# One core of Trainium2, a two-layer diffusion step with expert retrieval: GpSimd issues the last stage's rows without waiting for earlier ones to land, from places that open earlier

## The chip, the cores and the metric

The kernel runs on one core of a Trainium2 chip. The metric is the device time of one execution in microseconds. The engines are named as the profile names them: PE (TensorE), DVE (VectorE), ACT (ScalarE), POOL (GpSimd) and SP (SyncE, which here only starts transfers).

## What is computed

The reference is one inference step of a backbone with two layers. Each layer runs over a context of 128 tokens and over 256 latent tokens, width 1024, in f32. A layer mixes tokens (pooling windows, a scan, attention) and then retrieves experts:

```python
def peer_ffn(h, lp):
    ...
    q = (xt @ lp["peer_wq"]).reshape(n_tok, PEER_HEADS, 2, PEER_HALF)
    s = jnp.einsum("thmd,mhnd->thmn", q, lp["peer_keys"]).astype(jnp.float32)
    v1, i1 = lax.top_k(s[:, :, 0], PEER_TOPK)
    v2, i2 = lax.top_k(s[:, :, 1], PEER_TOPK)
    ...
    top_s, pos = lax.top_k(cand_s, PEER_TOPK)
    idx = jnp.take_along_axis(cand_i, pos, axis=-1)
    ...
        act = jnp.einsum("td,thkd->thk", xb, u_tab[ib])
        return jnp.einsum("thk,thkd->td", jax.nn.gelu(act) * gb, v_tab[ib])
```

Every token picks 128 of 16384 experts (8 heads, 16 each). For each pick it needs a row u of 1024 numbers (a dot product with the token, then gelu and gate) and a row v of 1024 numbers (added up with that weight). The pooling mixer subtracts each token from its mean over windows of 2, 4, 8 and 16 tokens. The outputs are the normed tokens and the new keys, values and scan states.

## The kernel before, in words

**Steps.** The program is four steps k = 0 to 3: context and latent of layer 0, context and latent of layer 1. A tile is 128 tokens, one per partition; a latent step has two tiles. A step has a dense part (projections, mixers, scores, the choice of experts) and a gather part. The gather part of a step lies partly beside the dense part of the next: `gather_plans` writes, for each named pause of the dense part, which gather events each engine does there, and `run_beside` carries that out on PE, ACT and DVE alike. `BESIDE_LATENT` is such a table: "s6" at the pause ("choose", 1, 0) means that share 6 of the weights is made there, "v24" that PE adds up four rows there.

**Rows and places.** POOL issues one indirect transfer per pick: it brings for each of the 128 tokens one row of the expert table (L825). For context steps these are single rows ("u" and "v", 128x1024); for latent steps they are double rows ("f", 128x2048), u and v side by side, about 1 MB a transfer. The last step has 256 of them, f0 to f255. A row lands in a place: a piece of `ring` (five double places), or memory that a stage doesn't need and lends with `spare_line` between two positions of the stream: pieces of `work`, `lent_line`, `wring[1]`. In the last step the order of places is worked out once, when the program is built; a row takes the free place that was used longest ago.

**What POOL waits for.** Before a row it waits (a) until the row that held the place before has been used: `u_used` counts dot products on DVE, `v_used` sums on PE; (b) for what the first use of a lent place names; (c) for a bound on rows under way, `UNDER_WAY = 8` in single rows: with a double row, the row five before it must have landed (`landed_first`, semaphores `row_landed...`). In the last step f0 to f4 go to the ring. The three double places in `work` open at `after_step[3]`, that is with row 11 of the step, and wait for `cleaned`: ACT multiplies the old contents by zero (`L.worn`, L1622) after the second tile's experts are chosen (`picked`), since the last step leaves out some rows. `lent_line` opens at row 8, two double places in `wring[1]` at row 52, two more at row 174.

**Last step.** Its first 24 x 128 experts are not gathered; they are computed densely: PE jobs "ua" (L1243, weights `peer_us`), a selection (L1257, L2243 and L2245 with the small table `count`), and sums "n" (L1271, weights `peer_vs`, 12 loads of 1 MB into two halves of `wring[0]`). For the picks that fall there the indirect transfer has an index out of bounds and moves nothing.

**A row's way.** DVE takes the dot product (L2229), ACT the gelu of two of them (L1630), DVE makes the weights of the two rows (L2185, L2193: `cond<-const,wv`), PE adds both up (L1287, `acc<-...,cond`), which frees the places. The engines run the events in the order of the plan; `events_two` writes it.

**SP.** At the end it loads `final_norm_w` for the context tile into hn[2], and later once more for the latent tiles into mod_a, then `count`, then `peer_vs`. Earlier it loads the band matrices of the pooling mixer, 128x2048 in a latent step, which PE multiplies at L1030 (one 256-column product for each of four windows and two tiles).

## Time and profile before

| | us |
|---|---|
| median of 3 runs | 2503.35 (2500.39 to 2504.37) |
| time of the profiled execution | 2499.15 |
| its span | 2497.0 |
| busy PE, DVE, POOL, ACT in the span | 1817.0, 1628.9, 999.7, 358.8 |

```profile
DMA  9989999979889999999999999987997999999997
GB/s 382 406 349 357 385 397 328 351 307 368 299 355 422 423 415 421 421 416 422 422 390 421 383 403 374 352 333 283 351 345 285 383 377 396 374 365 376 391 395 281
...
q0 software_dynamic: 147456, 740.81, 75.5%
q1 hardware_dynamic: 19490, 187.93, 18.4%
```

The span is cut into 40 slices of 62.4 us; a digit of DMA is the busy share of the 16 DMA engines in tenths. The lower two lines are queues: packets, MB and share; q0 carries POOL's rows, q1 what SP starts. The last step's rows are added up from about 1892 us to 2485 us, slices 31 to 40.

### The profile page before, as it was taken

Reading aid. Unit: us, or ns where it says so; the run is one execution under the profiler, and the core shown is the slowest. Engines: PE = TensorE matmul, PEld = TensorE weight load, DVE = VectorE, ACT = ScalarE, POOL = GpSimd, SP = SyncE. Lnnn points to the kernel's source line nnn. Section 1 sums busy time; section 2 is a strip of 40 time slices with the busy share of each in tenths; the row PEclk is TensorE's granted clock in tenths of the full one; section 3 lists DMA queues with packets and bytes.
Section 4 is the critical chain, followed back from the end, with each engine's and each line's share of the span. In section 5 each row is a group of like instructions: output and inputs, shape, how many; then the busy total and the mean of one; then the engine's idle time right before and its main releaser. Section 6 shows DMA issues by size and latency. Waiting matters only on the chain.

```text
span 2497.0 us, 24844 instructions
## 1 busy us (share of the span) xinstructions
PE 1817.0 (73%) x7834; PEld 840.7 (34%) x7834; DVE 1628.9 (65%) x4613; ACT 358.8 (14%) x1003; POOL 999.7 (40%) x1028
## 2 busy tenths in 40 slices
PE   6899656778447576676646796677985978778995
PEld 2455432354112221123311264235641533333221
DVE  0348984574785456564588689456666669887557
ACT  1321132101010122210001113211111000000000
POOL 0004536544533233333333555644453445444343
PEclk9899788978678787888977898787997989989998
DMA  9989999979889999999999999987997999999997
GB/s 382 406 349 357 385 397 328 351 307 368 299 355 422 423 415 421 421 416 422 422 390 421 383 403 374 352 333 283 351 345 285 383 377 396 374 365 376 391 395 281
DMA packets 167076, 930.31 MB, mean 373 GB/s; under 512 B 26311, under 2 KB 28871, under 8 KB 97007
## 3 DMA queue, kind: packets, MB, share of 16 engines
q0 software_dynamic: 147456, 740.81, 75.5%
q1 hardware_dynamic: 19490, 187.93, 18.4%
q8 instruction: 62, 1.02, 0.2%
q14 instruction: 68, 0.56, 0.1%
HBM read 990.08 MB, written 3.15 MB: 398 GB/s over the span
## 4 chain that ended last, share of the span: by engine, by line
DMA 31%; PE 29%; DVE 18%; issue 14%; another core or an unknown queue 4%; ACT 3%; POOL 1%; SPq 0%; POOLq 0%; DVEq 0%; ACTq 0%
DMA ring<-peer_uv_in,vidx 14%; DMA work<-peer_uv_in,vidx 11%; PE psum L1193 7%; PE acc L1287 5%; PE acc L1309 3%; PE psum L917 3%; DMA wring<-peer_uv_in,vidx 2%; DVE work L2229 2%; DVE ring L2281 2%; DVE work L1733 1%; PE psum L944 1%; PE psum L1243 1%; DVE work L1728 1%; PE acc L843 1%
## 5 line engine op out<-in xcount | busy, mean ns | idle before, releaser
L825 POOL DMA_INDIRECT ring<-peer_uv_in,vidx x428 | 419.2, 979 | 598.8 <-PE acc L1287 194.8
L1287 PE MATMUL acc<-ring,cond 128*32 128x512 f32 x984 | 294.0, 709 | 225.0 <-DVE cond L2193 222.7
L825 POOL DMA_INDIRECT ring<-peer_uv_in,idx x193 | 182.8, 947 | 379.5 <-DVE idx L1865 201.9
L825 POOL DMA_INDIRECT work<-peer_uv_in,vidx x207 | 205.4, 992 | 285.2 <-PE acc L1287 99.2
L2229 DVE CUSTOM_DVE_ANT_0 work<-work,h_kept 128x1024 f32<-128x1024 f32 (+1 forms) x183 | 221.2, 1218 | 98.3 <-DMA work<-peer_uv_in,vidx 92.3
L1287 PE MATMUL acc<-work,cond 128*32 128x512 f32 x732 | 213.3, 695 | 67.3 <-DVE cond L2193 66.3
L2281 DVE CUSTOM_DVE_ANT_0 ring<-ring,h_kept 128x1024 f32<-128x1024 f32 x193 | 224.1, 1216 | 8.5 <-DMA ring<-peer_uv_in,idx 4.1
L2229 DVE CUSTOM_DVE_ANT_0 ring<-ring,h_kept 128x1024 f32<-128x1024 f32 x128 | 153.9, 1218 | 75.5 <-DMA ring<-peer_uv_in,vidx 59.2
L1193 PE MATMUL psum<-work,wring 128*128 128x256 f32 (+1 forms) x896 | 172.8, 353 | 29.2 <-issue 26.2
L1287 PEld LDWEIGHTS acc<-ring,cond 128*32 128x32 f32 x984 | 53.0, 122 | 414.2 <-DVE cond L2193 262.6
L1630 ACT ACTIVATE dots<-dots 128x2 f32<-128x2 f32 x256 | 51.9, 203 | 917.4 <-DVE dots L2229 911.6
L2229 DVE CUSTOM_DVE_ANT_0 work<-ring,h_kept 128x1024 bf16<-128x1024 f32 x118 | 142.5, 1217 | 54.0 <-DMA ring<-peer_uv_in,vidx 39.0
L1309 PE MATMUL acc<-ring,lent_line 128*32 128x512 f32 x728 | 126.3, 700 | 66.5 <-DVE lent_line L2176 34.7
L1193 PEld LDWEIGHTS psum<-work,wring 128*128 128x128 f32 x896 | 148.7, 201 | 58.2 <-issue 39.0
L1351 ACT ACTIVATE work<-psum 128x512 f32<-128x512 f32 (+3 forms) x226 | 94.5, 429 | 509.8 <-PE psum L1193 150.6
L917 PE MATMUL psum<-wring,work 128*128 128x512 f32 (+1 forms) x400 | 153.6, 540 | 10.1 <-ACT work L1382 5.7
L1287 PEld LDWEIGHTS acc<-work,cond 128*32 128x32 f32 x732 | 41.7, 122 | 211.5 <-issue 106.2
L1728 DVE MAX8 work<-work 128x8 f32<-128x128 f32 (+1 forms) x288 | 52.5, 253 | 83.5 <-ACT work L1351 67.4
L917 PEld LDWEIGHTS psum<-wring,work 128*128 128x128 f32 x400 | 72.2, 198 | 92.3 <-issue 84.9
L825 POOL DMA_INDIRECT lent_line<-peer_uv_in,vidx x57 | 56.3, 987 | 92.9 <-PE acc L1287 46.7
L1271 PE MATMUL psum<-wring,work 128*128 128x512 f32 x192 | 92.9, 620 | 0.0
L1243 PE MATMUL psum<-work,wring 128*128 128x256 f32 x384 | 88.8, 385 | 0.3 <-issue 0.3
(280 smaller groups left out, 2674.5 us busy)
## 6 DMA issues: line engine op xcount, KB each, us to landing
wring<-w_in_in SPq DMA_DIRECT2D x17, 2048.0 KB
wring<-peer_wq_in SPq DMA_DIRECT2D x14, 2048.0 KB
wring<-mod_w_in SPq DMA_DIRECT2D x10, 2048.0 KB
ring<-mod_w_in SPq DMA_DIRECT2D x9, 2048.0 KB, 11.8
wring<-w_out_in SPq DMA_DIRECT2D x8, 2048.0 KB
wring<-peer_us_in SPq DMA_DIRECT2D x6, 2048.0 KB
wring<-peer_vs_in SPq DMA_DIRECT2D x12, 1024.0 KB, 9.3
work<-mod_w_in SPq DMA_DIRECT2D x5, 2048.0 KB, 14.1
```

Source lines behind the costliest of these rows:

```text
L825: nc.gpsimd.indirect_dma_start(row(kind, k, t, r)[0], None, io["peer_both" if kind == "f" else "peer_one"], bass.IndirectOffsetOnAxis(ap=a ...
L917: ins = mm(p[:, 0:n], st.L.hT[0][:, b, t * P:(t + 1) * P], w[:, b, slot:slot + n], start=(b == 0), stop=(b == DB - 1))
L1193: ins = mm(p[:, 0:N], chunk("wq", k, b // 4)[:, kb, (b % 4) * P:(b % 4 + 1) * P], st.L.hT[1][:, kb, 0:N], start=(kb == 0), stop=(kb == DB ...
L1243: ins = mm(p[:, 0:st.N], w[:, b, i % PER_CHUNK * P:(i % PER_CHUNK + 1) * P], st.L.hT[1][:, b, 0:st.N], start=(b == 0), stop=(b == DB - 1))
L1271: ins = mm(bank("vd", k, 2 * t + half)[:, :], steps[k].L.expert_acts[:, i, t * P:(t + 1) * P], shared_v(part)[:, at:at + CHUNK], start=(i ...
L1287: ins = mm(acc[half][lane:lane + QUAD, :], vw_duo(k, t, i)[:, j * QUAD:(j + 1) * QUAD], held[:, D + half * CHUNK:D + (half + 1) * CHUNK], ...
L1309: ins = mm(acc[half][lane:lane + QUAD, :], w[:, at:at + QUAD], two[j - pair][0][:, half * CHUNK:(half + 1) * CHUNK], start=(r == 0), stop= ...
L1351: A(dst, src, ACT.Copy, scale=scale).then_inc(*take(*key))
L1630: A(dots[:, at:at + DUO], dots[:, at:at + DUO], ACT.Gelu_apprx_tanh).then_inc(*mark("gelu", k, t, i))
L1728: d(V.max(top[:, b * TOPK + 8 * r:b * TOPK + 8 * r + 8], values[:, b * width:(b + 1) * width]))
L2229: V.tensor_tensor_reduce(st.L.products[i % 2] if st.dense else held[:, 0:D], held[:, 0:D], h_kept[:, :], 1.0, 0.0, ALU.mult, ALU.add, dots ...
L2281: V.tensor_tensor_reduce(held, held, h_kept[:, :], 1.0, 0.0, ALU.mult, ALU.add, dots[:, dots_at(k, t) + r:dots_at(k, t) + r + 1]).then_inc ...
```

## The change

It has seven parts.

1. In the last step POOL does not wait for an earlier row to have landed: `if n in landed_first and not steps[k].dense`. In the other steps it still does.
2. Places of the last step: the three double places in `work` and `lent_line` open at row 5 or 8 (`INDEXED_ROW`, `CLEANED_ROW`) in place of 11 and 8. Two of them (10D to 14D) wait for `both_indexed` of the second tile and for the first `cleaned`; the third (8D to 10D) for `picked` of the second tile and the second `cleaned`. The places behind, and how many there are, stay as they were.
3. ACT's cleaning is cut in two events "c": the first, 128x1512, at the pause ("choose", 1, 0), the second, 128x2048, at ("exp", 1). Before, two of 128x2048 came with the event "S".
4. Shares 6 and 7 of the context step's weights are made earlier, at ("choose", 0, 7) and ("choose", 1, 0) in place of ("choose", 1, 0) and ("choose", 1, 2).
5. On DVE and POOL's list, row f2's dot product comes behind the weights of rows 0 and 1.
6. The bands of a latent step shrink from 2048 to 1088 columns (`REACH` = 136): only the part of each window matrix that is not zero is loaded and multiplied. PE does 12 products (136, 16 and 120 columns) where it did 8 of 256.
7. SP: the final norm's weights are loaded once, into hn[2], and used for all three tiles. In step 0 the first chunk of `peer_wq` is loaded behind the states' output and the keys, not ahead of them.

```diff
+REACH = 128 + max(POOL_WINDOWS) // 2
...
+INDEXED_ROW, CLEANED_ROW = 5, 8
...
-            L.band = region(10776, 2048)
+            L.band = region(10776, 8 * REACH)
...
-                L.worn = [region(8 * D, 2 * D), region(12 * D, 2 * D)]
+                L.worn = [region(12824, 14 * D - 12824), region(8 * D, 2 * D)]
...
-        spare_line(region(10 * D, 2 * D), 2, after_step[STEPS - 1], len(stream))
-        for worn in steps[STEPS - 1].L.worn:
-            spare_line(worn, 2, after_step[STEPS - 1], len(stream))
+        indexed_used, cleaned_used = row_no["f", STEPS - 1, 0, INDEXED_ROW], row_no["f", STEPS - 1, 0, CLEANED_ROW]
+        spare_line(region(10 * D, 4 * D), 4, indexed_used, len(stream))
+        spare_line(region(8 * D, 2 * D), 2, cleaned_used, len(stream))
...
-        line_from = {k: row_no["f", k, 0, LENT_ROW] for k in (1, 3)}
+        line_from = {1: row_no["f", 1, 0, LENT_ROW], 3: row_no["f", 3, 0, INDEXED_ROW]}
...
-                    load_chunk("wq", k, 0)
...
                 for cc in range(4):
-                    if k or cc:
-                        load_chunk("wq", k, cc)
+                    load_chunk("wq", k, cc)
...
-                if st.lat:
-                    sp.wait_ge(*after("h2", st.k, st.T - 1))
-                else:
+                if not st.lat:
...
-                if n == after_step[STEPS - 1]:
-                    pool.wait_ge(*after("cleaned"))
+                if n == indexed_used:
+                    pool.wait_ge(*after("both_indexed", STEPS - 1, 1))
+                    pool.wait_ge(*after("cleaned", 0))
+                if n == cleaned_used:
+                    pool.wait_ge(*after("picked", STEPS - 1, 1))
+                    pool.wait_ge(*after("cleaned", 1))
...
-                if n in landed_first:
+                if n in landed_first and not steps[k].dense:
                     pool.wait_ge(*row(*stream[landed_first[n]])[1:])
...
+                        near, far = (st.L.band[:, (g * T + ti) * REACH:(g * T + ti + 1) * REACH] for ti in range(T))
+                        both = 2 * REACH - N
+                        mm(to[:, 0:REACH], held[0], near, start=True, stop=False)
+                        mm(to[:, N - REACH:REACH], held[1], far[:, 0:both], start=False, stop=True)
+                        ins = mm(to[:, REACH:N], held[1], far[:, both:], start=True, stop=True)
...
+                if kind == "c":
+
+                    act.wait_ge(*after("picked", k, i))
+                    worn = steps[k].L.worn[i]
+                    A(worn, worn, ACT.Copy, scale=0.0).then_inc(*mark("cleaned", i))
...
+BESIDE_DENSE = {("choose", 0, 7): "v23 s6", ("choose", 1, 0): "v24 v25 s7", ("choose", 1, 2): "v28 v29"}
...
+            if steps[k].dense:
+                plan["choose", 1, 0] = plan["choose", 1, 0] + [("c", k, 0, 0)]
+                plan["exp", 1] = plan["exp", 1] + [("c", k, 1, 1)]
+                third = left.pop(left.index(("f", k, 0, 2)))
+                left.insert(left.index(("p", k, 0, 0)) + 1, third)
```

**POOL at the start of the last step's rows**, in the kernel before. A row is an instruction: line, kind, place and table, shape, and the semaphores it waits for; `row_landed` with a number is the landing of an earlier row, `v_used` the sums on PE. The first row is f0:

```order
L825 DMA ring<-peer_uv_in,vidx 128x2048 [waits v_used,row_landed45,both_indexed]
L825 DMA ring<-peer_uv_in,vidx 128x2048 [waits row_landed2,v_used]
...
L825 DMA ring<-peer_uv_in,vidx 128x2048 [waits row_landed4,v_used]
L825 DMA lent_line<-peer_uv_in,vidx 128x2048 [waits v_used,row_landed6,mod_whole]
...
L825 DMA work<-peer_uv_in,vidx 128x2048 [waits row_landed2,cleaned,picked]
```

And in the changed kernel, from f0:

```order
L829 DMA ring<-peer_uv_in,vidx 128x2048 [waits v_used,both_indexed]
L829 DMA ring<-peer_uv_in,vidx 128x2048 [waits v_used] x4
L829 DMA work<-peer_uv_in,vidx 128x2048 [waits v_used,mod_whole,cleaned,both_indexed]
L829 DMA work<-peer_uv_in,vidx 128x2048
L829 DMA lent_line<-peer_uv_in,vidx 128x2048 [waits v_used]
L829 DMA work<-peer_uv_in,vidx 128x2048 [waits cleaned,picked]
L829 DMA ring<-peer_uv_in,vidx 128x2048 [waits v_used] x2
```

Rows f5 to f8 have moved from ring and `lent_line` places, which wait for sums of this step's own rows, to `work` and `lent_line`, which wait for none of them; the waits for landings are gone from every row of the step.

**DVE while the last step's experts are chosen**, before (L1871 is the end of the first tile's choice, L1886 waits for ACT's exp, L2176 makes a share of weights):

```order
L1871 COPY vidx<-idx 32x32 x15
L1880 COPY small<-work 128x8
L1882 TENSOR_TENSOR work<-work,small 128x128 [waits v_step]
L1886 TENSOR_REDUCE small<-work 128x8 [waits topk_exp]
...
L1740 MATCH_REPLACE work<-work 128x128 x15
L2176 TENSOR_TENSOR lent_line<-const,wv 128x512 [waits v_used,v_step]
```

and in the changed kernel:

```order
L1882 COPY vidx<-idx 32x32 x15
L1891 COPY small<-work 128x8
L1893 TENSOR_TENSOR work<-work,small 128x128 [waits v_step]
L2187 TENSOR_TENSOR lent_line<-const,wv 128x512 [waits v_used]
L1897 TENSOR_REDUCE small<-work 128x8 [waits topk_exp]
...
L1751 MATCH_REPLACE work<-work 128x128 x15
L2187 TENSOR_TENSOR lent_line<-const,wv 128x512 [waits v_used,v_step]
```

Share 6 now stands ahead of the wait for `topk_exp`, and share 7 where share 6 was.

**DVE at the last step's first rows**, before (L2309 ends the context tile's sum, the ISA rows are dot products, L2185 and L2193 make the weights of rows 0 and 1):

```order
L2309 TENSOR_TENSOR x2<-x2,acc1 64x512 x2
L2229 ISA work,dots<-ring,h_kept 128x1024 [waits x_new,v_step,u_used,row_landed4]
L2229 ISA dots 128x1
L2185 TENSOR_TENSOR wv<-dots,idx 128x2 [waits gelu]
L2193 TENSOR_TENSOR cond<-const,wv 128x64 [waits v_used,v_step]
```

and in the changed kernel:

```order
L2320 TENSOR_TENSOR x2<-x2,acc1 64x512 x2
L2196 TENSOR_TENSOR wv<-dots,idx 128x2 [waits x_new,v_step,gelu]
L2204 TENSOR_TENSOR cond<-const,wv 128x64 [waits v_used,v_step]
L2240 ISA work,dots<-ring,h_kept 128x1024 [waits u_used,row_landed4]
L2240 ISA dots 128x1
```

The dot product of f2 has moved behind the weights that PE waits for.

## Rows read from the trace of the kernel before

**Rows 1.** Windows: length, busy PE, PEld, DVE, ACT, POOL; clock, DMA share, GB/s.
```profile
1905.00:1950.00 45.00, 34.43 (x146) 18.31 (x147) 24.58 (x53) 3.56 (x15) 20.53 (x21) 0.92 0.96 367
1950.00:2200.00 250.00, 200.17 (x943) 94.21 (x941) 195.52 (x444) 14.89 (x65) 117.65 (x113) 0.91 0.98 383
2100.00:2200.00 100.00, 80.30 (x404) 37.04 (x404) 85.75 (x189) 5.67 (x24) 50.64 (x48) 0.92 0.97 380
2200.00:2300.00 100.00, 81.78 (x383) 33.24 (x384) 87.45 (x195) 5.29 (x26) 48.15 (x46) 0.92 0.95 363
2300.00:2480.00 180.00, 158.24 (x480) 46.62 (x476) 111.22 (x248) 7.52 (x37) 71.28 (x71) 0.96 0.98 390
```

**Rows 2.** The chain that ended last: the first of nine row transfers, 2092 to 2188 us.
```profile
2092.09 8.71 DMA ring<-peer_uv_in,vidx
```

**Rows 3.** POOL's line, 2090 to 2190 us: whom it waited for, us, times.
```profile
  PE acc L1287: 17.2, 15
  DMA ring<-peer_uv_in,vidx: 13.7, 10
  DMA work<-peer_uv_in,vidx: 8.4, 7
```

**Rows 4.** Windows in which the DMA engines had little to do.
```profile
1840.00:1850.00 10.00, 6.20 (x32) 1.35 (x32) 9.93 (x64) 0.00 (x0) 3.06 (x4) 0.51 0.49 179
1890.00:1905.00 15.00, 4.35 (x11) 1.14 (x11) 11.62 (x30) 4.04 (x4) 1.25 (x2) 0.52 0.26 88
```

**Rows 5.** Timeline of POOL: a slow issue, f4 and f5; start, duration, [idle before].
```profile
1873.41 2.88 POOL L825 DMA_INDIRECT ring<-peer_uv_in,vidx  x1 [0.30 <-issue]
...
1887.01 0.99 POOL L825 DMA_INDIRECT ring<-peer_uv_in,vidx  x1 [0.30 <-issue]
1903.03 0.99 POOL L825 DMA_INDIRECT ring<-peer_uv_in,vidx  x1 [15.03 <-PE acc L1287]
```

**Rows 6.** Timeline of DVE and ACT: both_indexed, picked, f2's dot product, the cleaning.
```profile
1883.34 0.29 DVE L1865 SCALAR_TENSOR_TENSOR idx<-work 128x128 uint32<-128x128 f32 x1
...
1888.90 0.29 DVE L1897 SCALAR_TENSOR_TENSOR cond<-work 128x128 f32<-128x128 f32 x1
...
1898.61 1.22 DVE L2229 CUSTOM_DVE_ANT_0 work<-ring,h_kept 128x1024 bf16<-128x1024 f32 x1 [0.28 <-DVE x L2309]
...
1895.11 3.69 ACT L1622 ACTIVATE work<-work 128x2048 f32<-128x2048 f32 x2
```

**Rows 7.** Timeline of PE: wait for share 6, the last context rows, the first sums.
```profile
1843.80 1.06 PE L1309 MATMUL acc<-ring,lent_line 128*32 128x512 f32 x1 [6.90 <-DVE lent_line L2176]
...
1882.94 1.94 PE L1309 MATMUL acc<-ring,lent_line 128*32 128x512 f32 x8 [2.60 <-DMA ring<-peer_uv_in,vidx]
...
1900.32 3.63 PE L1287 MATMUL acc<-ring,cond 128*32 128x512 f32 x8 [11.74 <-DVE cond L2193]
```

**Rows 8.** SP's transfers at 2005 to 2030 us: count, KB each, us from issue to landing.
```profile
y_prompt_out<-x SPq DMA_DIRECT2D x1, 512.0 KB, 4.5
mod_a<-final_norm_w_in SPq DMA_DIRECT2D x1, 512.0 KB, 9.5
...
work<-count_in SPq DMA_DIRECT2D x1, 64.0 KB, 11.4
```

**Rows 9.** Waits of 2000 to 2300 us: who, for whom, us, times, longest.
```profile
DVE work L2243 <- DMA work<-count_in: 9.6, 1, 9.6
```

**Rows 10.** SP's transfers at 2290 to 2430 us, and the first and last issue among them.
```profile
wring<-peer_vs_in SPq DMA_DIRECT2D x10, 1024.0 KB, 9.2
...
2297.12 11.27 SPq L641 DMA_DIRECT2D wring<-peer_vs_in  x2
...
2421.27 0.33 SPq L641 DMA_DIRECT2D wring<-peer_vs_in  x1
```

**Rows 11.** The band products of step 3, in the chain that ended last.
```profile
1511.25 3.71 PE psum L1030 x16
```

**Rows 12.** Step 0: issue of the first chunk of peer_wq, and PE's use of it.
```profile
148.68 0.33 SPq L657 DMA_DIRECT2D wring<-peer_wq_in  x1
...
164.34 10.98 PE L1193 MATMUL psum<-work,wring 128*128 128x128 f32 x96 [0.80 <-ACT work L1351]
```

More of the change, by code:

```diff
@@ L168, in shape_constants @@
             bands.append(b.reshape(length // P, P, length).transpose(1, 0, 2).reshape(P, -1))
-    lat = np.concatenate(bands[:4], 1).astype(np.float32)
+    lat = np.concatenate([band[:, ti * 2 * P:(ti + 1) * 2 * P][:, ti * (2 * P - REACH):][:, :REACH]
+                          for band in bands[:4] for ti in range(2)], 1).astype(np.float32)
     ctx = np.concatenate(bands[4:], 1).astype(np.float32)
@@ L1028, in dense @@
                         g = 2 * pair + r
[L1029 to L1031 removed]
+                        to = p[64 * r:64 * r + 64, :]
+                        held = [st.L.pz[ti][:, g * 64:(g + 1) * 64] for ti in range(T)]
+                        if T == 1:
+                            ins = mm(to[:, 0:N], held[0], st.L.band[:, g * N:(g + 1) * N], start=True, stop=True)
+                            continue
+                        near, far = (st.L.band[:, (g * T + ti) * REACH:(g * T + ti + 1) * REACH] for ti in range(T))
[3 more added lines that the diff above has]
+                        ins = mm(to[:, REACH:N], held[1], far[:, both:], start=True, stop=True)
                     ins.then_inc(*made("pl", k, pair))
@@ L1618, in gather @@
                 if kind == "S":
-                    if t == 0:
-                        act.wait_ge(*after("picked", k, 1))
-                        for j, worn in enumerate(steps[k].L.worn):
-                            ins = A(worn, worn, ACT.Copy, scale=0.0)
-                        ins.then_inc(*mark("cleaned"))
                     act.wait_ge(*after("picked", k, 1))
```

13 lines of the change are left out of this document (5 added, 8 removed).

## The prediction

> **What bounds the kernel now.** I read the slices first: in the last quarter of the span no compute engine is full and the DMA engines are at nine tenths almost throughout. Then the windows of the last stage [rows 1]: the DMA share is 0.96 to 0.98 from 1905 to 2200 us and again from 2300 to 2480 us, PE stands at 77 to 88% and DVE at 55 to 87%. Then the chain that ended last [rows 2]: from 2092 to 2188 us it is nine row transfers of about 9 us, one issued when the one five before it has landed, so about 2 us a row. That looks like a limit on rows under way, and POOL's waits name it too [rows 3]: 22 us in 100 for landings in the two rows shown, against 17.2 us for places. But with the DMA engines 97% busy at that time, a landing comes late because the engines are full, not because too little is asked of them. What an unbounded queue can win there is the missing 3%. From 2200 to 2300 us the share is 0.95 and the chain goes through DVE (dot product, selection, dot product): DVE sets the pace there, all places are full, and no queue helps.
>
> The last view is the windows with a low share [rows 4]: from 1890 to 1905 us the engines are 26% busy, 11.1 us of nothing; from 1840 to 1850 us 49% busy, 5.1 us. The cause of the first is in POOL's timeline [rows 5]: f0 to f4 fill the five ring places by 1888 us, and f5 is issued at 1903.03 after an idle 15.03 us, released by PE's first sum, which starts at 1900.32 [rows 7].
>
> So I keep the account in DMA time. The last stage must move a fixed number of bytes; it ends earlier by what the engines are spared or are kept busy more, as long as PE and DVE can follow.
>
> **The change part by part.**
>
> *Four rows earlier (parts 2 and 3).* f5, f6 and f7 need both_indexed, which DVE marks at 1883.6 us [rows 6], the end of the context rows' sums, 1884.9 us [rows 7], and the first cleaning, done long before; f8 needs the end of the choice, 1889.2 us, and the second cleaning, half of 3.69 us [rows 6], so about 1891. POOL needs 1.3 us an issue [rows 5], so all four are issued by 1893 us, when the kernel before stood idle until 1903. f9 then waits for ring place 0, as f5 did. Nine rows are there or under way at 1903 us where five were. A row costs the DMA engines 100 us x 0.97 / 48 = 2.02 us [rows 1], so four rows are **8.1 us**. Bounds: 0, if the stage were not bound by DMA; 11.1 us, the whole idle time of that window. I take 8.1, since the share right behind it is 0.96. Can PE and DVE follow? From 1905 to 1950 us PE is 77% busy and DVE 55% [rows 1], waiting for rows; with four rows more in hand these waits close. The cleaning moves on ACT and is smaller (1512 and 2048 columns for twice 2048); ACT is idle there: 0.
>
> *Shares 6 and 7 earlier (part 4).* PE waits 6.90 us for share 6 [rows 7], which starves POOL of places and makes the half-idle 1840 to 1850 us [rows 4]. Its removal brings the last context rows and f0 to f4 some 5 us forward. DVE's choice, on which the next step hangs, doesn't wait for them, and only nine places exist: I give it **0** beyond what it does for the four rows, namely that the queue is empty when f5 comes. If it counts in full it is 5.1 us, below nothing only by the 0.7 us that a share takes on DVE.
>
> *f2 behind the weights (part 5).* PE's first sum waits for DVE, and one dot product of 1.22 us [rows 6] leaves its front: ring place 0 comes free 1.2 us earlier while the DMA engines have nothing: **1.2 us**, bounds 0 and 1.2.
>
> *No bound on rows under way (part 1).* Nothing is added; a wait goes. What is late next is the place (PE's sum). The idle shares outside DVE's stretch are 0.04 x 45 + 0.02 x 250 + 0.02 x 180 = 10.4 us [rows 1]. The bound asks for a row to be whole, that is for the slowest of 16 engines, and the indices out of bounds spread the load unevenly from row to row; with up to nine or eleven rows queued in place of five a fast engine runs dry less often. But some of the idle time is places. Ends: 0 and 10.4; I take half, **5.2 us**.
> The Trainium skill (DMA: Bandwidth & Descriptors, Latency and other measured facts) says that two of the sixteen engines are usually slower than the rest. By that rule the slow ones would set the pace whatever the depth, this term would be 0 and the sum 12.1 us; no row here tells engines apart, and it is the second case below.
>
> *The second load of the norm's weights (part 7)* is 0.5 MB of 390 GB/s: **1.3 us** of DMA time. Also `count` stands behind it in SP's queue: they land 9.5 and 11.4 us after their issue [rows 8], and DVE waits 9.6 us for `count` [rows 9]. It will be about 5 us sooner (4.5 us for the output ahead of it, then 1.9, the difference of the two). DVE gains 4.9 us, but rows go on landing meanwhile and the DMA share is 0.98: **0**, at most 4.9.
>
> *The bands (part 6).* In step 3 the products stand in the chain, 3.71 us [rows 11]. Columns go from 2048 to 1088, to 0.53, instructions from 8 to 12: about 2.0 us, so up to 1.7 us; the loads shrink by 0.5 MB twice, 1.3 us each. Both lie before other waits. Bounds 0 and 3.0, I take **1.5**.
>
> *peer_wq in step 0.* It is issued at 148.68 us and used at 164.34 [rows 12]. Now it goes out about 1.7 us later and behind 1 MB of keys, 2.6 us. A 1 MB load lands in 9.2 us under full load [rows 10]; 2 MB add 2.6 us: 150.4 + 11.8 = 162.2. Covered by 2 us, so **0**; if the cover were short, 2 to 3 us lost.
>
> **Sum:** 8.1 + 1.2 + 5.2 + 1.3 + 1.5 = 17.3 us. The profiled execution took 2499.15 us (span 2497.0), so the same one would take 2481.9. The median of the runs is 4.2 us above the profiled one; from it: 2503.35 - 17.3 = **2486.0 us**.
>
> One thing could spoil the first term. One of POOL's issues takes 2.88 us in place of 0.99 while DVE works on 2048 columns [rows 5]. The new issues fall into DVE's copies of the indices; there f4's took 0.99. Should all four take 2.88, the last would be out at about 1897 us and landed before f9's place is free, a loss of 1 to 3 us.
> The Trainium skill (SBUF — State Buffer, two separate sides) has this as a rule: DVE's f32 copies lock GpSimd out of a shared port, and its transfers starve. By it the slow case holds, and the sum is 15 us.
>
> **The rivals.**
>
> *Depth is worth nothing, part of the rest is absorbed.* The idle 2 to 4% is unevenness that no depth cures, and the four rows bring only what PE's clock and ACT let through. For it: the share is near full. Gain 8 to 12 us, 2493 us.
>
> *All is recovered.* DVE's stretches start earlier by the count's 4.9 us as well and the share goes to 1.00: 17.3 + 5.2 + 4.9 = 27 us, 2476 us. Against it: both can't be had in full, since DMA and DVE take turns.
>
> *The lead is lost.* The four rows only fill places sooner, and DVE's stretch from 2200 us, 87% busy with its waits on ACT and PE between, or PE's from 1930 to 2000, sets the end. Gain under 5 us, 2501 us. Against: DVE's stretch starts only when a DMA-bound one ends [rows 2].
>
> *SP's loads stand behind the deep queue* (slower). If a load had to wait for all rows queued ahead of it, its landing would grow with the depth. peer_vs has two halves, and loads follow each other every (2421.27 - 2297.12) / 9 = 13.8 us [rows 10]; it lands in 9.2 us. From a landing above 13.8 us PE stops at each of ten loads. With nine rows at 2 us ahead, 18 us: 10 x 4.2 = 42 us lost, 2528 us with the gains taken off. Against it: with five rows, 10 us of work, under way, the 0.5 MB output landed in 4.5 us [rows 8], so the two queues take turns.
> The Trainium skill (DMA: Bandwidth & Descriptors, Queues, rings and completion order) says so too: each DMA engine goes round its queues packet by packet. The row agrees, and by the rule this case is excluded.
>
> *The change doesn't do what it says.* POOL may be held by the places at once, so that no more than five are ever under way. Then term 5.2 is 0, which is the first rival.
>
> **How the numbers follow.** A measurement of this kernel can tell about 0.2%, 5 us, from no change. Chances: forecast (2480 to 2490) 0.57; first rival 0.20; all recovered 0.10; lead lost 0.09; slower 0.04. Faster by over 0.2% is 0.87, within 0.2% 0.09, slower 0.04. The range leaves out the slower case and the edge of the others: from 2475 (all recovered) to 2500 (nearly all of the lead lost).
>
> **What would show it.** In the profile after: f5 to f8 issued between 1884 and 1893 us, POOL's wait ahead of f9 down to some 8 us, the share from 1890 to 1905 us near 0.7; no wait of 6.9 us for share 6; no landings among POOL's releasers in the last step, places in their stead; DMA share 0.98 to 0.99 where it was 0.96 to 0.98; DVE's wait for count near 5 us; vs loads landing in 9 to 10 us. I am wrong if the shares stay and the end moves by less than 8 us, if POOL's issues grow long (its descriptors find no room), or if PE waits for peer_vs.

## The result, and the profile after it

The changed kernel takes 2490.66 us (median of 20 runs, 2479.32 to 2509.22), the kernel before, run beside it, 2508.96 us (median of 20, 2498.27 to 2521.19). The measured ratio is 0.9935, with a 95% interval of [0.9917, 0.9953]: 16.3 us faster, 12 to 21 (the two medians alone are 18.3 us apart). The forecast was 17.3 us faster, and 2486.0 us as a time. The time came out 4.7 us above that, inside the stated range of 2475 to 2500 but just outside its likeliest part, 2480 to 2490, because the forecast started from a median of three runs, 2503.35 us, that lies 5.6 us below the median of 20.

Single executions of one kernel lie up to 19 us from their median, so two profiled ones can't be subtracted: the one of the changed kernel took 2494.02 us (span 2492.1) and was already 12.2 us behind at the last step's first peer_us load (1768.72 us, 1756.53 in the kernel before), although the code up to there differs in little. I therefore measure from two marks that every profile has: **approach**, from that load's issue to PE's first sum of the last stage, and **stage**, from that sum to the end of the span. Before: 143.8 and 596.7 us. After: 139.7 and 583.7 us.

Windows of the kernel after, for [rows 1, 4]; the columns are as there.

```profile
1852.20:1862.20 10.00, 5.74 (x32) 3.22 (x32) 8.58 (x54) 0.00 (x0) 6.49 (x7) 0.98 1.01 405
1898.11:1913.11 15.00, 4.46 (x11) 1.14 (x11) 12.72 (x34) 2.93 (x6) 4.25 (x5) 0.51 0.68 245
...
1840.00:1850.00 10.00, 10.00 (x64) 6.80 (x60) 8.12 (x50) 4.69 (x7) 3.96 (x6) 1.00 1.04 416
1890.00:1905.00 15.00, 1.56 (x2) 0.00 (x0) 13.21 (x49) 4.25 (x6) 6.00 (x7) 0.50 0.93 330
...
2100.00:2200.00 100.00, 83.90 (x372) 37.64 (x372) 78.74 (x171) 5.15 (x22) 46.52 (x43) 0.83 0.94 369
2200.00:2300.00 100.00, 83.99 (x385) 34.08 (x386) 88.88 (x198) 5.28 (x26) 52.86 (x50) 0.92 0.93 361
2300.00:2400.00 100.00, 95.84 (x284) 29.45 (x283) 53.14 (x116) 4.07 (x20) 41.29 (x43) 0.98 1.01 413
2400.00:2480.00 80.00, 66.37 (x207) 18.23 (x207) 58.27 (x132) 3.66 (x18) 25.78 (x26) 0.91 0.86 345
```

The same times on the clock don't hold the same work here: the changed kernel is 12.2 us late at the load and 8.1 us late at the first sum, so its rows for 1840 and 1890 us show work that the kernel before did 8 to 12 us earlier. The first two rows are the matching stretches, shifted by 12.2 us for the first hole and laid from 10.3 us ahead of the first sum to 4.7 us behind it for the second. The first hole is closed, 1.01 for 0.49. The second is narrowed: 0.68 for 0.26, near the 0.7 that was foretold, so 4.8 us of idle time are left of 11.1; the 0.93 of the unshifted row is no measure of it. From 2300 to 2400 us the engines move 413 GB/s; the same window of the kernel before reads

```profile
2300.00:2400.00 100.00, 92.93 (x275) 28.71 (x272) 53.82 (x119) 3.86 (x19) 38.61 (x39) 0.98 0.98 391
```

From 2200 to 2300 us, DVE's stretch, nothing is gained, as the prediction had it. The last row of the first fence is new: 0.86 near the end, where the kernel before has 0.97 from 2400 to 2480 us, because the last rows have landed by about 2470 us and the rest of that window has nothing to move.

The bytes show the four rows too. From the load to the first sum the engines of the kernel before move 324 GB/s over 143.8 us, 46.6 MB, and those of the kernel after 356 GB/s over 139.7 us, 49.7 MB; from the first sum to the end it is 368 GB/s and 219.6 MB before, 370 GB/s and 216.0 MB after. Three to four megabytes have moved ahead of the first sum.

POOL's timeline of the kernel after, for [rows 5]: f3 to f9.

```profile
1890.36 0.99 POOL L829 DMA_INDIRECT ring<-peer_uv_in,vidx  x1 [0.30 <-issue]
1891.65 0.99 POOL L829 DMA_INDIRECT ring<-peer_uv_in,vidx  x1 [0.30 <-issue]
1896.85 0.99 POOL L829 DMA_INDIRECT work<-peer_uv_in,vidx  x1 [4.21 <-DVE vidx L1882]
1898.15 0.99 POOL L829 DMA_INDIRECT work<-peer_uv_in,vidx  x1 [0.30 <-issue]
1899.44 0.99 POOL L829 DMA_INDIRECT lent_line<-peer_uv_in,vidx  x1 [0.30 <-issue]
1901.55 1.00 POOL L829 DMA_INDIRECT work<-peer_uv_in,vidx  x1 [1.12 <-ACT work L1630]
1911.12 0.99 POOL L829 DMA_INDIRECT ring<-peer_uv_in,vidx  x1 [8.57 <-PE acc L1299]
```

f5 to f8 go out at 1896.85 to 1901.55 us (12.2 us less for the late start: 1884.7 to 1889.4), one wait each for the index copies (DVE, L1882, which mark both_indexed) and for the second cleaning, and 8.57 us ahead of f9 in place of 15.03 ahead of f5. PE's wait for share 6 is gone: from 1820 to 1880 us none of its waits in the kernel after names DVE. PE's first sum:

```profile
1908.41 3.63 PE L1299 MATMUL acc<-ring,cond 128*32 128x512 f32 x8 [16.84 <-DVE cond L2204]
```

Waits of POOL in the kernel after, 1950 to 2400 us (us, times, longest): no landing among the long ones, places throughout.

```profile
POOL ring L829 <- PE acc L1299: 88.8, 40, 5.1
POOL work L829 <- PE acc L1299: 60.4, 23, 7.7
POOL ring L829 <- issue: 17.8, 50, 0.7
POOL lent_line L829 <- PE acc L1299: 16.0, 8, 6.4
POOL wring L829 <- PE acc L1299: 14.7, 12, 2.2
```

What an unbounded queue does to one row, in the chain that ended last of the kernel after: its three transfers from 2300 to 2400 us. In the kernel before there are six in that stretch, of 9.1 to 15.9 us (the nine of about 9 us that the prediction went by stood from 2092 to 2188 us).

```profile
2304.64 25.63 DMA ring<-peer_uv_in,vidx
...
2348.16 24.04 DMA ring<-peer_uv_in,vidx
...
2386.52 22.56 DMA work<-peer_uv_in,vidx
```

A row takes 23 to 26 us from issue to landing, and the kernel is faster. DVE waits 1.8 us for count, 9.6 before [rows 9]:

```profile
DVE work L2254 <- DMA work<-count_in: 1.8, 1, 1.8
```

### The profile page after: what moved, and what is told of

The parts are those of the page before. It is cut to its first block, busy times and chain, and to the rows that moved or that the text cites. A ratio compares the mean times of both kernels' runs of the same rounds, so it can differ in the third digit from the quotient of the medians.

```text
span 2492.1 us, 24631 instructions
## 1 busy us (share of the span) xinstructions
PE 1832.2 (74%) x7850; PEld 845.1 (34%) x7850; DVE 1629.4 (65%) x4613; ACT 358.0 (14%) x1003; POOL 1004.0 (40%) x1028
## 3 DMA queue, kind: packets, MB, share of 16 engines
q1 hardware_dynamic: 19346, 186.42, 18.3%
## 4 chain that ended last, share of the span: by engine, by line
PE 29%; DMA 27%; DVE 22%; issue 12%; another core or an unknown queue 5%; ACT 3%; POOL 1%; SPq 0%; DVEq 0%; POOLq 0%; ACTq 0%
DMA ring<-peer_uv_in,vidx 14%; DMA work<-peer_uv_in,vidx 9%; PE acc L1299 7%; PE psum L1205 6%; PE psum L921 3%; DVE ring L2292 2%; DVE work L1744 2%; DVE work L2240 2%; PE psum L948 2%; DVE work L1739 2%; PE acc L1321 1%; PE psum L1255 1%; DMA wring<-peer_uv_in,vidx 1%; DVE work L1751 1%
## 5 line engine op out<-in xcount | busy, mean ns | idle before, releaser
L1299 PE MATMUL acc<-work,cond 128*32 128x512 f32 x740 | 219.5, 701 | 65.9 <-DVE cond L2204 64.2
L1321 PE MATMUL acc<-ring,lent_line 128*32 128x512 f32 x728 | 121.0, 689 | 52.5 <-DVE lent_line L2187 27.3
L2196 DVE TENSOR_TENSOR wv<-dots,idx 128x2 f32<-128x2 f32 x256 | 40.0, 156 | 83.3 <-ACT dots L1641 81.5
```

What stands on the lines that cost most here:

```text
L1299: ins = mm(acc[half][lane:lane + QUAD, :], vw_duo(k, t, i)[:, j * QUAD:(j + 1) * QUAD], held[:, D + half * CHUNK:D + (half + 1) * CHUNK], ...
L1321: ins = mm(acc[half][lane:lane + QUAD, :], w[:, at:at + QUAD], two[j - pair][0][:, half * CHUNK:(half + 1) * CHUNK], start=(r == 0), stop= ...
```

## The experiments

All of them were timed in five rounds; a1 to a4 share their runs of the kernel before, as do the repeated kernel and b1 to b3, and d1 to d3 and c1, which ran on another chip. Their intervals are 0.2 to 0.35% wide to each side, 5 to 9 us, so each verdict takes the stage and the approach of the profile with it. All in one table:

| kernel | ratio to before [95%] | approach | stage |
|---|---|---|---|
| before | 1 | 143.8 | 596.7 |
| changed | 0.9935 [0.9917, 0.9953] | 139.7 | 583.7 |
| changed, again | 0.9926 [0.9899, 0.9953] | 139.3 | 576.5 |
| a1: bound back | 0.9937 [0.9903, 0.9971] | 139.3 | 590.7 |
| a2: before + bound off | 1.0007 [0.9977, 1.0036] | 142.5 | 591.4 |
| a3: places late | 0.9958 [0.9927, 0.9988] | 144.1 | 591.4 |
| a4: shares late | 0.9928 [0.9900, 0.9956] | 143.9 | 583.3 |
| b1: second norm load | 0.9943 [0.9922, 0.9964] | 139.0 | 586.5 |
| b2: whole bands | 0.9908 [0.9882, 0.9934] | 139.8 | 583.5 |
| b3: bound of 3 rows | 1.0403 [1.0380, 1.0426] | 139.7 | 696.3 |
| d1: bound back, places late | 0.9960 [0.9936, 0.9985] | 138.5 | 599.2 |
| d2: bound off and places alone | 0.9945 [0.9915, 0.9974] | 143.0 | 580.9 |
| d3: bound of 4 rows | 1.0017 [0.9992, 1.0043] | 140.3 | 607.3 |
| c1: no bound anywhere | 0.9938 [0.9907, 0.9969] | 140.3 | 578.5 |

**How far one profile carries.** The changed kernel, unedited.

> The changed kernel once more, unedited, to see how far one profile's stages can be trusted. 'Stage' here is the time from the issue of the first peer_us load of the last step to the end of the span: 740.5 us in the kernel before, 723.4 in the changed one, 730.0 with the bound back, 733.9 with the bound off alone, 735.5 with the places late, 727.2 with the shares late. If the stage repeats to 2 us (727 or less, 721 or more), the differences of 4 to 12 us between these profiles are effects of the edits; if it comes out at 728 or more, single profiles can't carry them. Ratio to the kernel before 0.9935 again, within 0.003.

It came out at 715.8 us (139.3 + 576.5), 7.6 less than its first profile: below the limit of 721 that I had set. The approach repeats to 0.4 us, the stage does not. With the kernels that have both the absent bound and the places (changed twice, a4, b1, b2, d2, c1) the stage reads 576.5 to 586.5 us, mean 581.8: a single one is good to some 5 us.

**Bound back (part 1 undone).**

```diff
-                if n in landed_first and not steps[k].dense:
+                if n in landed_first:
```

> The changed kernel with the bound of five rows under way put back in the last stage (part 1 undone), all else as changed. The changed kernel is 16 us faster than the one before (ratio 0.9935). Prediction's theory (depth is worth half of the idle shares, 5 us): 11 us faster than the kernel before, ratio 0.9955, and in the stretch from 2300 to 2400 us the DMA engines move about 391 GB/s again as in the kernel before, where the changed kernel moved 413; POOL's releasers are landings again. Rival 'depth is worth nothing' (the rate would follow the rows that the stage happens to ask for): ratio stays at 0.9935, and the rate there stays above 405. Rival 'depth is nearly the whole gain' (the rate rose by 5%, so 5% of some 280 us of full DMA engines, 14 us): ratio 0.998 to 1.000. If the loads of peer_vs stood behind the deep queue, PE's waits on them would shrink here; none is seen in the changed kernel, so no change is expected.

Windows of this kernel, in the same columns:

```profile
1890.00:1905.00 15.00, 7.78 (x26) 2.85 (x27) 11.66 (x23) 0.79 (x3) 3.16 (x5) 0.64 0.67 244
...
2300.00:2400.00 100.00, 95.00 (x282) 29.12 (x281) 54.90 (x121) 4.07 (x20) 39.54 (x40) 0.98 0.98 394
```

The rate is back at 394 GB/s, so it follows the depth and not the rows asked for, and landings are POOL's releasers again:

```profile
POOL ring L829 <- DMA work<-peer_uv_in,vidx: 28.7, 16, 3.2
```

The stage is 8.9 us over the mean of the seven kernels with both parts. But the runs show a ratio of 0.9937, no loss against 0.9935 and 0.9926; 0.9955 lies inside the interval too. This profile started its peer_us load within 0.2 us of the kernel before, and shows the share of 0.67 that was foretold for 1890 to 1905 us (near 0.7), without any shift.

**Bound off alone.** The same line, changed in the kernel before.

> The kernel before with nothing changed but that POOL keeps no bound on rows under way in the last stage (part 1 alone). Prediction's theory: 5 us faster, ratio 0.998; f5 still goes out at about 1903 us (places alone hold it), and the rows after 1910 us are issued as places come free. Rival 'depth is worth nothing': within 1 us, ratio 1.000, DMA rate from 2300 to 2400 us at 391 GB/s. Rival 'depth is nearly the whole gain': 12 to 15 us faster, ratio 0.9945, the rate at 413 GB/s. Rival 'places limit it anyway' (change does not do what it says): single rows would take no longer than the 9 us of the kernel before from issue to landing, where the changed kernel shows 15 to 25 us.

```profile
2300.00:2400.00 100.00, 95.58 (x284) 29.00 (x284) 53.85 (x118) 3.86 (x19) 41.53 (x42) 0.98 1.01 413
```

The rate is 413 GB/s without any other part, and the stage 5.3 us shorter than before. The runs show 1.0007: the expected 0.998 is just inside, 12 to 15 us are out.

**Places late (part 2 undone).**

```diff
-INDEXED_ROW, CLEANED_ROW = 5, 8
+INDEXED_ROW, CLEANED_ROW = 11, 11
...
-        line_from = {1: row_no["f", 1, 0, LENT_ROW], 3: row_no["f", 3, 0, INDEXED_ROW]}
+        line_from = {1: row_no["f", 1, 0, LENT_ROW], 3: row_no["f", 3, 0, LENT_ROW]}
```

> The changed kernel with rows f5 to f8 given no places of their own before f11 (part 2 undone: the double places of indexed_used, cleaned_used and the lent line are used from row 11 on), all else as changed. Prediction's theory (four rows are 8.1 us of DMA time): 8 us slower than the changed kernel, that is 8 us faster than the kernel before, ratio 0.9967; the stretch from 1890 to 1905 us shows a DMA share near 0.3 again. Rival 'the lead is lost' (rows earlier only fill places sooner, DVE or PE sets the end): ratio 0.9935 as the changed kernel, though the hole at 1890 to 1905 us is back. Rival 'the hole counts in full and the first sums are delayed too' (11 us and more): ratio 0.998 or above.

The hole is back, here as POOL's wait ahead of f5, and as the stretch that matches 1890 to 1905 us of the kernel before:

```profile
1903.33:1918.33 15.00, 4.46 (x11) 1.16 (x11) 12.69 (x35) 3.29 (x6) 1.27 (x2) 0.50 0.06 8
...
1916.35 0.99 POOL L829 DMA_INDIRECT ring<-peer_uv_in,vidx  x1 [23.72 <-PE acc L1299]
```

It is deeper than before, a share of 0.06 where near 0.3 was expected. A likely reason is that with the shares made early (part 4) the rows ahead of it have landed sooner, which leaves 3 us more of idle time for the four rows to fill. The stage is 9.6 us over the mean of the seven, the ratio 0.9958. Both stand nearer to 8 us of loss than to none; the lost-lead rival falls by the stage, the runs alone would leave it open. Its approach of 144.1 us is the one outlier of that column, and I have no cause for it.

**Shares late (part 4 undone).**

```diff
-    texts = BESIDE_LATENT | BESIDE_EARLY if early else BESIDE_LATENT | BESIDE_OPENING | {"dt": "u11"} | BESIDE_DENSE
+    texts = BESIDE_LATENT | BESIDE_EARLY if early else BESIDE_LATENT | BESIDE_OPENING | {"dt": "u11"}
```

> The changed kernel with the shares 6 and 7 of the gated and summed rows beside the choice left where they were before (part 4 undone). Prediction's theory (worth 0): ratio 0.9935 as the changed kernel, though PE waits some 7 us for share 6 again and the DMA share from 1840 to 1850 us is near 0.5. Rival 'counts in full': the time from the issue of the first peer_us load to PE's first sum of the last stage is 4 us longer (143.8 us before, 139.7 after), and the ratio is 0.995.

PE's longest wait from 1820 to 1880 us of this kernel, as in [rows 7]:

```profile
PE acc L1321 <- DVE lent_line L2187: 6.9, 1, 6.9
```

The wait is back as expected. The share came out at 0.66, not near 0.5, in the stretch that matches 1840 to 1850 us (1847.80 to 1857.80 us here). The approach is 143.9 us. It is 142.5 to 143.9 in all four kernels with the late shares (before, a2, a4, d2) and 138.5 to 140.3 in nine of ten with the early ones: the rival was right, the part brings the first sum forward by 4 us. Whether the end follows can't be read: the ratio says no, and 4 us are inside its interval. The kernel also settles the rival on SP's queue. Its transfers, with no bound on rows:

```profile
wring<-peer_vs_in SPq DMA_DIRECT2D x12, 1024.0 KB, 9.1
```

The kernel before has 9.3 us in that row of its page. A load doesn't stand behind 25 us of rows.

**Second norm load.** 0.5 MB ahead of count, unused.

```diff
+                    sp.wait_ge(*after("h2", st.k, st.T - 1))
+                    load(mod_a[:, :], final_w, "fw_in", "again")
                     sp.wait_ge(*after("picked", st.k, st.T - 1))
                     load(st.L.count, io["count"], "count_in")
```

> The changed kernel with the last step's second load of the norm's weights (0.5 MB) put back ahead of count, into a tile that nobody reads afterwards. Prediction's theory: 1.3 us of DMA time and DVE's wait for count longer by some 5 us (1.8 us in the changed kernel, 7 to 8 here), worth 0 to 4.9 us, so the stage (first peer_us load to the end) is 1 to 3 us longer than 723.4 and the ratio 0.994. Rival 'the wait for count counts in full': the choice after it and the rows behind are late by the whole 5 us, stage 729 to 730, ratio 0.996.

```profile
DVE work L2256 <- DMA work<-count_in: 10.1, 1, 10.1
```

The wait is 10.1 us, longer than expected; the ratio 0.9943 and stage 586.5 (4.7 over the mean) fit 1 to 3 us and don't exclude 5. Over all profiles the wait for count is 7.8 to 11.1 us with the load (before, a2, b1, d2) and 1.8 to 7.3 us, mean 5.1, without it (ten): "near 5" holds only as a mean.

**Whole bands (part 6 undone).** The matrices of 256 columns a block are loaded and multiplied again, in two matmuls in place of three.

```diff
-            L.band = region(10776, 8 * REACH)
+            L.band = region(10776, 2048)
...
-                        mm(to[:, 0:REACH], held[0], near, start=True, stop=False)
-                        mm(to[:, N - REACH:REACH], held[1], far[:, 0:both], start=False, stop=True)
-                        ins = mm(to[:, REACH:N], held[1], far[:, both:], start=True, stop=True)
```

> The changed kernel with the whole bands of the pooling windows loaded and multiplied (part 6 undone: 2048 columns for 1088, 0.5 MB more in each latent step). Prediction's theory: 1.5 us, ratio 0.994; nothing changes behind the first peer_us load of the last step, so the stage is 723 to 725 us as in the changed kernel. Rival (all 3 us of it count, and more where the loads stand before the first dense work): ratio 0.9955; the stage still the same.

0.9908, the lowest ratio of all, though more work is done. Its interval overlaps that of the changed kernel, so I don't call it faster; but 3 us of loss are excluded and 1.5 lies at the edge: the term is about 0.

**Bound of three double rows.** The last stage's limit at half its value.

```diff
-            while behind and under_way + size[stream[behind - 1][0]] <= UNDER_WAY:
+            most = 4 if stream[n][1] == SHARED_STEP else UNDER_WAY
+            while behind and under_way + size[stream[behind - 1][0]] <= most:
...
-                if n in landed_first and not steps[k].dense:
+                if n in landed_first:
```

> The changed kernel with a bound in the last stage of three double rows under way, where the kernel before has five and the changed one none. Theory 'depth fills the DMA engines': the rate in the stretch from 2300 to 2400 us went from 391 GB/s (bound of five) to 413 (none); with three it falls to 350 or less, and the stage is 745 us or more (11% fewer bytes a second over the 280 us in which the engines are full is 30 us, part of it hidden), ratio 1.003 to 1.01. Rival 'the end hangs on PE and DVE, depth only moves the same bytes forward': the rate falls but the stage grows by no more than the 7 us that the bound of five costs it, ratio below 0.998.

```profile
2300.00:2400.00 100.00, 82.07 (x263) 27.10 (x264) 54.73 (x119) 3.67 (x18) 37.05 (x38) 0.90 0.92 327
```

The rival falls. 327 GB/s, a stage of 696.3 us and 4.0% more than the kernel before: far above what I expected of the first theory, whose direction is right. Depth is worth much here as long as it is scarce. In its chain (22 transfers from 2100 to 2400 us) a row lands in 5.2 to 10.0 us.

**Both large parts undone, and both alone.** d1 joins the edits of a1 and a3; d2 joins those of a4, b1 and b2, puts f2 back before the weights and the first chunk of peer_wq of step 0 back ahead of the keys.

```diff
-                third = left.pop(left.index(("f", k, 0, 2)))
-                left.insert(left.index(("p", k, 0, 0)) + 1, third)
...
                     modulation(MOD_AT["mid"])
+                    load_chunk("wq", k, 0)
```

> The changed kernel with both large terms undone together: the bound of five rows is back and rows f5 to f8 have no places before f11; the small parts 4 to 7 stay as changed. Prediction's sum (5.2 + 8.1 = 13.3 us of 17.3 gone): 4 us faster than the kernel before, ratio 0.9984. Rival 'the two terms overlap' (each undone alone showed 0 to 8 us over the changed kernel in whole runs, but they serve the same rows): with both gone the loss is larger than the sum of the two, ratio 1.000. Rival 'the small parts carry most of it' (shares and f2 earlier, count sooner; a loss of only some 5 us here): ratio 0.995.

> The complement: the changed kernel with parts 4 to 7 undone (shares 6 and 7 and f2 where they were, whole bands, the second load of the norm's weights ahead of count, peer_wq's first chunk of step 0 early), so that of the change only the absent bound and the four places are left. Prediction's sum: 13.3 us faster than the kernel before, ratio 0.9947, and the first peer_us load to first sum takes 143 to 144 us as before. Rival 'the small parts carry most of it': ratio 0.998. Rival 'the small parts are worth nothing together': ratio 0.993 as the changed kernel.

d1's windows show the hole (0.07 of share; its first sum is 1.9 us behind that of the kernel before) and the old rate:

```profile
1890.00:1905.00 15.00, 2.81 (x8) 0.64 (x8) 13.58 (x40) 4.25 (x6) 0.10 (x1) 0.50 0.07 28
...
2300.00:2400.00 100.00, 95.41 (x283) 29.22 (x282) 54.49 (x117) 4.07 (x20) 38.79 (x40) 0.98 0.98 391
```

d2 is where the sum put it, 0.9945 for 0.9947. d1 is at 0.9960 for 0.9984: by it the parts 4 to 7 carry 10 us of 16 rather than 4, though 0.9984 is still inside the interval. d2, which leaves them out, is only 2 to 5 us slower than the changed kernel. The stage of d1, 599.2 us, is near that of the kernel before (596.7), as it should be with both parts gone; the parts 4 to 7 shorten d1's approach by 5.3 us.

**Bound of four double rows.** As b3, with 6 in place of 4.

> The changed kernel with a bound of four double rows under way in the last stage. With three the kernel took 1.0403 of the kernel before (some 117 us more than the changed one) and the rate in 2300 to 2400 us was 327 GB/s; with five 0.9937 and 394; with none 0.993 and 413. Theory 'a landing takes about as long whatever the depth, so rows under way over that time is the rate, until the engines are full': three rows gave 327, four give some 380 to 390, and the loss is 15 to 35 us, ratio 1.000 to 1.007. Rival 'a threshold between three and five': as with five, ratio 0.995 or less, or as with three, above 1.02.

```profile
2300.00:2400.00 100.00, 93.61 (x272) 28.65 (x270) 52.09 (x114) 3.86 (x19) 37.70 (x38) 0.97 0.97 375
```

375 GB/s, a little under the 380 to 390 expected, and the ratio within its range: no threshold, a curve that flattens. The reason given for the range is wrong, though: a landing doesn't take about as long whatever the depth. In the chains from 2300 to 2400 us it is 5.2 to 10.0 us at three rows, 9.8 to 10.9 at four, 9.1 to 15.9 at five (before) and 22.6 to 25.6 with no bound (after).

**No bound in any step.**

```diff
-                if n in landed_first and not steps[k].dense:
+                if n in landed_first and False:
```

> The changed kernel with the bound on rows under way gone in all steps, not in the last alone: a candidate for a faster version. In the steps before the last the slices show DMA shares of 0.98 and up with 421 to 423 GB/s over long stretches with the bound in place, so little is left to win: theory gives the same time as the changed kernel, ratio 0.992 to 0.995. Rival 'depth fills the engines in the thinner stretches too': 5 to 10 us less, ratio 0.989 to 0.991. Rival 'weights stand behind the rows': PE waits longer for weight loads in the dense parts of steps 1 to 3, ratio above 0.997.

The same time as the changed kernel. No cost of the bound shows in the earlier steps (the interval, 0.9907 to 0.9969, leaves room for some us either way), and no version was found that beats the changed kernel for certain.

## Why the prediction was right, and where it wasn't

To set the runs against the sum, I fitted three terms (part 1, parts 2 and 3, parts 4 to 7) to the seven ratios that are combinations of them (changed twice, a1, a2, a3, d1, d2), each weighted by its interval and taken as independent, though those of one round share their runs of the kernel before, and the stages beside them:

| term | predicted | from the runs, 95% | from the stages |
|---|---|---|---|
| no bound (1) | 5.2 | 0.8, -4 to 5.6 | 6.6 to 8.9 |
| four rows (2, 3) | 8.1 | 8.8, 3.2 to 14.4 | 7.3 to 9.6 |
| parts 4 to 7 | 4.0 | 8.2, 3.9 to 12.5 | outside the stage |

A fit to the single executions, with a level for each round's kernel before, has the same middles, 0.7, 9.8 and 7.8 us, with 3.0, 3.5 and 3.0 us to each side. If the executions of a round are independent of one another, that puts 5.2 us outside for the bound and 4.0 just outside for parts 4 to 7.

The stages' figures: without bound, places missing, 591.4 (a2, a3) against 598.0 (mean of before and d1): 6.6; with places, 581.8 against 590.7 (a1): 8.9. For the places 598.0 - 590.7 = 7.3 and 591.4 - 581.8 = 9.6.

- **Four rows, 8.1 us: right**, by mechanism and size. POOL's wait ahead of f9 is 8.57 us for 8, the share in the hole 0.68 for 0.7, and the value of a row, the 2.02 us of DMA time it takes, fits what was measured. One mark was misread: both_indexed isn't marked at 1883.6 us, the end of L1865, but by the 16 copies behind it (L1871, until 1887.1 us), and POOL's wait ahead of f5 in the kernel after ends with those copies. It did no harm, since f4's issue kept POOL until 1888.0 us in the kernel before, and since the copies end some 3 us sooner, counted from the load, in the kernel after. Whether PE and DVE could follow was asked there: they do. From 5 to 50 us behind the first sum the share is 0.98 in the changed kernel, 0.97 in the kernel before.
- **No bound, 5.2 us: the mechanism is right, the size stays open.** The rate rises with depth in every profile: 391, 394 and 391 GB/s with five rows (before, a1, d1), 410 to 414 in the nine without bound. It isn't SP's share of the window: POOL's rows alone are 31.20 MB in it before and 32.87 MB after. The step "what an unbounded queue can win there is the missing 3%" is too small: the share rose from 0.98 to 1.01, 3%, and the rate by 5.6%. On the time, runs and stages disagree by 6 to 8 us; 5.2 lies inside the interval from the ratios, and within the scatter of 5 us of single profiles. By the runs nothing at all may be left of this term: a1 loses no time that they can see, and a2 gains none. Part of the gap is that the profiles without bound happened to start the first peer_us load late (mean 1765.6 us in nine, 1757.5 in the five with bound), in a stretch whose rows keep the bound in all but c1. The lateness builds up slowly, 2 us at the first load of the cached keys, 7 us at the second and 8 at peer_us. I know no mechanism for that; it may be chance, though it is large for that with 5 and 6 us of scatter inside the groups. Whether it belongs to the missing bound would decide between the two columns, and only more profiles could tell.
- Part of the higher rate is not cashed. From the issue of the last row to the end it is 22.0 to 26.9 us in the five profiles with a bound and 31.9 to 32.7 in the nine without: the last row is issued sooner and then waits its turn behind the others. The DMA engines are also done sooner, counted from the end: from 25 to 20 us ahead of it their share is 0.97 in the kernel before and 0.41 in the kernel after, with DVE 84 to 85% busy in both, so the rows are in and what is left there is work of DVE and PE. How much of the gain that costs was not tried. From the first sum to the last issue it is 571.7 us (mean of before and d1) with the bound and 559.1 without (a2, a3), 12.6 less; to the end it is 6.6 less.
- **Shares 6 and 7, 0 us: this step was wrong.** "DVE's choice doesn't wait for them" left out that the first sum hangs on the end of the context rows too; it comes 3.8 us sooner (mean of nine 139.5, of four 143.3), near the upper bound of 5.1. It is the only mark by which a part of 4 to 7 shows clearly, and the likeliest source of the 4 us by which these parts exceed their sum. That any of it reaches the end is argued, not shown: a4, with this part alone undone, has 0.9928, no loss.
- **f2 behind the weights, 1.2 us: not seen.** a4 has it and reaches the first sum in 143.9 us; without it 142.5 to 143.8 (before, a2, d2).
- **Bands, 1.5 us: not seen** (b2). **Norm weights, 1.3 us: fits** (b1: 0.8 to 1.7 thousandths over the changed kernel, 2 to 4 us, uncertain by some 7). **peer_wq, 0: nothing seen**; it wasn't tried alone.
- **The rivals.** "Depth is worth nothing" (8 to 12 us in all, 12 being the edge of the measured interval): the runs of a1 and a2 don't exclude it, but its reason, an unevenness that no depth cures, fell with the rate, and the share went to 1.01; "all is recovered" (27 us) is out; "lead lost" (under 5 us in all) is out by the result, which is 12 us or more; "SP's loads stand behind the deep queue" is out: peer_vs lands in 9.1 us. "Places hold POOL anyway" is out: rows of 25 us.
- The Trainium skill's rule on two slow engines (DMA: Bandwidth & Descriptors, Latency and other measured facts) had been read as a gain of nothing from depth. No run tells engines apart, so the rule stands; what I drew from it, a rate that doesn't move, fell.
- The sum came within 1 us of the measured difference by some luck: by the middles of the fit, parts 4 to 7 brought 4 us more than their terms and part 1 some 4 us less, and the two errors cancel.

## What to carry to other kernels

Where a queue of gathers is held to a fixed number under way, vary the number by one in both directions before arguing about it: the curve here costs the stage 114 us at three, 25 at four and 9 at the most at five (the whole runs say less), against no limit; a limit between five and none wasn't tried. A hole in which the DMA engines stand idle in a stage bound by transfers is worth the transfers that can be put into it, and can be costed as rows times the time a row takes. Where executions scatter more than the effect, measure in the profiles between marks that every version has, lay the windows that are compared from the same mark and not from the same time, repeat one version to learn how far one profile carries, and test complements (both parts off, both alone).

## What the runs showed of the hardware

**Depth against rate.** Rows of the software queue, each a gather of which part of the indices is out of bounds, from 2300 to 2400 us: three under way 327 GB/s (share 0.92), four 375 (0.97), five 391 to 394 (0.98), as many as places allow 410 to 414 (1.00 to 1.01). Stages: 696.3, 607.3, 590.7 and 581.8 us (mean). In the chains a row lands in 5.2 to 10.0 us at three, in 9.3 to 15.9 at five (a1), in 22.6 to 25.6 without bound from 2300 us on (after). Above five rows, where the share already read 0.98, the rate still rose by 5.6%; the unevenness of the 16 engines is the likely cause and wasn't measured.

**What slows POOL's issues.** The prediction feared DVE's work on 2048 columns and DVE's copies of the indices. DVE's timeline of the kernel after, beside POOL's two slow issues of that time:

```profile
1882.25 2.29 DVE L1852 TENSOR_TENSOR work<-work 128x2048 f32<-128x2048 f32 x1
1884.58 2.29 DVE L1847 TENSOR_REDUCE work<-work 128x128 f32<-128x2048 f32 x1
1886.90 2.29 DVE L1852 TENSOR_TENSOR work<-work 128x2048 f32<-128x2048 f32 x1
1889.22 2.29 DVE L1847 TENSOR_REDUCE work<-work 128x128 f32<-128x2048 f32 x1
...
1892.73 3.33 DVE L1882 COPY vidx<-idx 32x32 uint32<-32x32 uint32 x16
```

```profile
1882.68 2.73 POOL L829 DMA_INDIRECT ring<-peer_uv_in,vidx  x1 [2.15 <-PE acc L1321]
1885.72 1.00 POOL L829 DMA_INDIRECT ring<-peer_uv_in,vidx  x1 [0.30 <-PE acc L1321]
1887.02 3.03 POOL L829 DMA_INDIRECT ring<-peer_uv_in,vidx  x1 [0.30 <-issue]
```

The two slow ones began inside a TENSOR_TENSOR and ended 0.87 and 0.86 us after it (1884.54, 1889.19). Those that began inside a TENSOR_REDUCE of the same 2048 columns took 1.00 and 0.99 us (1885.72, and 1890.36 above). The repeated profile shows the same pair, 2.85 and 3.04 us. So it is the operation with two inputs, not its width. Which began first counts too: in the kernel before an issue at 1877.84 us, 0.01 us behind the start of such a TENSOR_TENSOR, took 1.00 us, and the next, at 1879.15 us and inside it, took 1.89. Two of the four new issues, at 1898.15 and 1899.44 us, ran beside 16 copies of DVE (L2229, 32x32 in f32, 1898.18 to 1901.89 us) and took 0.99 us each: the slow case that the prediction priced at 1 to 3 us did not come.
The Trainium skill (SBUF — State Buffer, Who interferes with whom) states this: `tensor_tensor` with both inputs in SBUF contends with GpSimd's reads, `tensor_reduce` never does on trn2. The rows agree. The same section infers that such an operation leaves GpSimd's descriptor generation alone; the slow issues above speak against that. The rule that the prediction took from an earlier section of that page does not hold for the 16 copies beside the new issues.
